# Query projection with stationary weights, an earlier start of the output projection, and an up projection ordered by weight part

## The chip, the core and the metric

The kernel runs on one core of a Trainium2 chip. A core has a matrix engine (TensorE, PE in the rows; PEld are its weight loads), a vector engine (DVE), a scalar engine (ACT), GpSimd (POOL) and a queue engine (SP) that issues the transfers from HBM. The engines run side by side and wait for each other by semaphores. The metric is the device time of one execution in microseconds (us), lower is better. A row's clock is the TensorE clock that was granted, as a share of full speed: 1.00 is 2.4 GHz, 0.50 is 1.2 GHz.

## What is computed

One decoder layer for 256 tokens of width 2048: attention in two families of heads, then an MLP, with RMS norms. Cut to what matters here:

```python
proj = rmsnorm(h, attn_norm_w) @ w_in            # 2048 -> latents, q_nsa (1024), kv (768), gates (48)
y_mla = mla_attention(c_q, c_kv, k_rope, ...)    # 8 heads, causal softmax
# nsa: 16 heads of 64; q = q_nsa.reshape(T, 2 groups, 8, 64)
s_c = q @ k_cmp.T / 8 - slope * dist             # 15 compressed blocks per group
o_c = softmax(s_c) @ v_cmp                       # "cmp"
o_s = softmax(q @ k_s.T / 8 - slope * dist) @ v_s   # "slc"; all blocks are selected at this length
o_w = softmax(q @ k_w.T / 8 - slope * dist) @ v_w   # "win"
y_nsa = g0 * o_c + g1 * o_s + g2 * o_w
h = h + concat(rmsnorm(y_mla), rmsnorm(y_nsa)) @ w_o
n = rmsnorm(h, mlp_norm_w)
h = h + square(relu(n @ w_up)) @ w_down          # 2048 -> 8192 -> 2048
return rmsnorm(h, final_norm_w)
```

## The kernel before

**Split operands.** Every large product is made in three parts. An operand is split into a rounded high part and the low rest (`w_hi`, `w_lo`; `xT[:, 0]`, `xT[:, 1]`), and the kernel adds high times high, high times low and low times high. Weights stream from HBM in chunks of 1 MB or a little less into four slots of `raw`; ACT makes `w_hi` (two slots), DVE then makes `w_lo` (two slots), and TensorE consumes the chunk. Semaphores: `hi_done` and `lo_done` count split chunks, `w_used` consumed ones, `w_half` half-consumed ones among chunks 21 to 27.

**Chunks.** Chunks 0 to 20 are the rest of the input projection and the MLA projections. Chunks 21, 23, 25, 27 (`CMP`) are the weights of the block compression. Chunks 22, 24, 26, 28, 29, 30, 31, 32 (`A_IN`) are the 1024 columns of NSA queries in `w_in`. Chunks 33 to 48 are the output projection (`WO_M` = 33 for the MLA half, `WO_N` = 41 for the NSA half), and from 49 on come the MLP's. `products` (L1199, L1200, L1203) keeps a token tile of 128 as the stationary operand and streams 512 weight columns; its result has tokens on partitions. `heads` (L1316 to L1318) does the reverse for MLA: 128 weight columns are stationary, the 256 tokens stream, and the result comes out turned, features on partitions. `up_products` (L1571, L1573) is of the second kind too: a wide matmul streams 512 columns, which are two strips of 256 (high and low part of `xT`) against `w_hi`, and a narrow one streams 256 against `w_lo`.

**Queries before.** All eight `A_IN` chunks add into PSUM banks 0 to 3 by `products`, each chunk carrying 256 rows of the weight and all 1024 columns. After chunk 32, ACT and DVE scale the two token tiles into `q_sb` (L673, L1004). TensorE then transposes it, 16 times (L1524, step `turn_q`), and ACT and DVE split each of the four banks into `q2` (L679 and L784, in turn, four times).

**Steps.** The attention is 48 steps, each a set of engine slots `("s", i)`. In slot i TensorE makes the scores of step i, transposes the probabilities of step i-3 (L1410), and multiplies those of step i-4 by the values (L1436, L1437). DVE takes the row minimum (L931) and scales the probabilities (L945, L946). ACT copies, takes exponentials, and for a finished unit writes `ysb`, `yT` and its square (L637, L639, L641); DVE adds the low part of `yT`. Steps 0 to 7 are MLA, 8 to 47 NSA (slc, win, slc, win, cmp for each pair of heads). `scores` are the 32 small products of all heads with the compressed keys (L1533, 32 columns each, into banks 2 and 3); `soft` reads them (L1015, L1016, then `cs_in`) and `weigh` finishes them. The NSA queries are needed from slot 8 on.

**Order.** `PLAN` is a list written out by the code at the top of the file that all engines run through: `("w", c)` is a chunk, `("q", (c, n))` a quarter of one (24 or, for a quarter, 6 matmuls), `("hi"/"lo", (c, half))` the splits, `("s", i)` a slot, `("k", name)` a named piece. A quarter of an output chunk is block n//2 for token tile n%2; tile 0 goes to banks 0 and 1, tile 1 to banks 2 and 3, so tile 1 has to wait for `cs_in`. The end of the attention norm (`norm_n`, L1368) goes through DVE and a chain of small POOL instructions (L416 to L419, L469) before DVE may add the first NSA half of the output projection (L970), which frees the banks for chunk 45.

**MLP.** 64 chunks of `w_up` and 64 of `w_down`; the first 8 of `w_up` are unrolled, the other 56 lie in a hardware loop of 7 rounds (`pe.Fori(1, G)`), in which 4 chunks up and 4 chunks down alternate. One up chunk is 4 banks (f) of 4 blocks (b), so 16 pairs of a wide and a narrow matmul.

## Time and profile before

| what | value |
|---|---|
| median of 3 runs | 1104.94 us (1104.5 to 1106.25) |
| the profiled execution, whole | 1105.58 us |
| its span, first to last instruction | 1103.6 us |
| PE busy | 1076.3 us (98%) |
| PE weight loads busy | 898.2 us (81%) |
| DVE, ACT, POOL busy | 635.5, 496.8, 97.4 us |
| mean granted TensorE clock | 0.993 |

The page's times are of one execution. The end of a matmul is modelled, so its busy time is no measure of how densely matmuls follow each other; for that the distance between starts in the timeline is read. A busy share is a mean over stages; the timeline and the chain of waits tell which stage waits for what. Roughly: input and MLA projections to 126 us, compression and queries with the MLA steps to 201, NSA steps with the output projection to about 346, the rest of the output projection to 380, MLP to the end.

### The profile page before, as it was taken

Reading aid. Unit: us, or ns where it says so; the run is one execution under the profiler, and the core shown is the slowest. Engines: PE = TensorE matmul, PEld = TensorE weight load, DVE = VectorE, ACT = ScalarE, POOL = GpSimd, SP = SyncE. Lnnn points to the kernel's source line nnn. Section 1 sums busy time; section 2 is a strip of 40 time slices with the busy share of each in tenths; the row PEclk is TensorE's granted clock in tenths of the full one; section 3 lists DMA queues with packets and bytes.
Section 4 is the critical chain, followed back from the end, with each engine's and each line's share of the span. In section 5 each row is a group of like instructions: output and inputs, shape, how many; then the busy total and the mean of one; then the engine's idle time right before and its main releaser. Section 6 shows DMA issues by size and latency. Waiting matters only on the chain.

```text
span 1103.6 us, 14211 instructions
## 1 busy us (share of the span) xinstructions
PE 1076.3 (98%) x5560; PEld 898.2 (81%) x5560; DVE 635.5 (58%) x781; ACT 496.8 (45%) x603; POOL 97.4 (9%) x159
## 2 busy tenths in 40 slices
PE   8999899999999999999999999999999999999996
PEld 7889787867777888888888888888888888888884
DVE  4655754677674655446545555555555654654565
ACT  4645444676654364334433433433433433443433
POOL 2136000322214000000000000000000000000003
PEclk9999999899999999999999999999999999999999
DMA  9576553142224556556555565565655555565552
GB/s 323 164 205 191 179 202 115 39 153 77 78 84 144 158 178 193 175 188 193 185 190 189 185 192 187 189 190 188 191 189 189 190 190 190 190 190 190 190 191 77
DMA packets 82977, 190.42 MB, mean 173 GB/s; under 512 B 8742, under 2 KB 21628, under 8 KB 82556
## 3 DMA queue, kind: packets, MB, share of 16 engines
q1 hardware_dynamic: 82508, 189.41, 53.9%
q10 hardware_dynamic: 432, 0.52, 0.2%
q8 instruction: 23, 0.38, 0.1%
q14 instruction: 14, 0.11, 0.0%
HBM read 187.82 MB, written 2.10 MB: 172 GB/s over the span
## 4 chain that ended last, share of the span: by engine, by line
PE 91%; DVE 5%; ACT 2%; issue 1%; DMA 0%; DVEq 0%; POOL 0%; ACTq 0%
PE ps L1571 21%; PE ps L1199 16%; PE ps L1200 16%; PE ps L1203 16%; PE ps L1573 11%; PE ps L1436 2%; DVE w_lo L784 1%; PE ps L1410 1%; ACT w_hi L529 1%; PE ps L1386 1%; PE ps L1437 1%; PE ps L1389 1%; PE ps L1385 1%; PE ps L1533 1%; PE ps L1390 1%
## 5 line engine op out<-in xcount | busy, mean ns | idle before, releaser
L784 DVE TENSOR_TENSOR w_lo<-raw,w_hi 128x2048 fp32r<-128x2048 f32 (+4 forms) x197 | 402.1, 2044 | 362.7 <-ACT w_hi L536 289.8
L536 ACT ACTIVATE w_hi<-raw 128x2048 fp32r<-128x2048 f32 x119 | 228.5, 1920 | 397.9 <-PE ps L1203 200.3
L1571 PE MATMUL ps<-xT,w_hi 128*128 128x512 f32 x1024 | 361.9, 398 | 1.3 <-DVE h_sb L970 1.0
L1573 PE MATMUL ps<-xT,w_lo 128*128 128x256 f32 x1024 | 287.4, 281 | 0.0
L1571 PEld LDWEIGHTS ps<-xT,w_hi 128*128 128x128 f32 x1024 | 192.3, 188 | 48.9 <-issue 1.3
L1573 PEld LDWEIGHTS ps<-xT,w_lo 128*128 128x128 f32 x1024 | 193.4, 189 | 0.5
L1200 PE MATMUL ps<-w_lo,hidT 128*128 128x512 f32 x448 | 174.5, 389 | 0.0
L1199 PE MATMUL ps<-w_hi,hidT 128*128 128x512 f32 x448 | 174.4, 389 | 0.0
L529 ACT ACTIVATE w_hi<-raw 128x1024 fp32r<-128x1024 f32 (+3 forms) x76 | 105.6, 1396 | 80.0 <-PE ps L1203 59.5
L1203 PE MATMUL ps<-w_hi,hidT 128*128 128x512 f32 x448 | 137.9, 389 | 0.0
L1199 PEld LDWEIGHTS ps<-w_hi,hidT 128*128 128x128 f32 x448 | 84.1, 188 | 17.7
L1203 PEld LDWEIGHTS ps<-w_hi,hidT 128*128 128x128 f32 x448 | 84.1, 188 | 17.6
L1200 PEld LDWEIGHTS ps<-w_lo,hidT 128*128 128x128 f32 x448 | 84.1, 188 | 17.0
L1199 PE MATMUL ps<-w_hi,xT 128*128 128x512 f32 (+2 forms) x184 | 68.7, 373 | 3.7 <-DVE w_lo L784 3.2
L498 POOL TENSOR_TENSOR h_sb<-h_sb,fw 128x1024 f32<-128x1024 f32 x2 | 6.2, 3111 | 724.0 <-ACT sink L745 724.0
L1200 PE MATMUL ps<-w_lo,xT 128*128 128x512 f32 (+2 forms) x184 | 65.6, 363 | 0.0
L1199 PE MATMUL ps<-w_hi,yT 128*128 128x512 f32 x128 | 55.0, 430 | 0.7 <-DVE h_sb L970 0.5
L1203 PE MATMUL ps<-w_hi,xT 128*128 128x512 f32 (+2 forms) x184 | 51.8, 363 | 0.0
L1200 PE MATMUL ps<-w_lo,yT 128*128 128x512 f32 x128 | 50.3, 393 | 0.0
L627 ACT ACTIVATE probT<-ps 128x384 f32<-128x384 f32 (+1 forms) x48 | 24.1, 502 | 53.5 <-PE ps L1410 43.1
L1199 PEld LDWEIGHTS ps<-w_hi,xT 128*128 128x128 f32 x184 | 34.5, 188 | 12.5 <-issue 4.7
L1203 PE MATMUL ps<-w_hi,yT 128*128 128x512 f32 x128 | 39.6, 391 | 0.0
(285 smaller groups left out, 1161.6 us busy)
## 6 DMA issues: line engine op xcount, KB each, us to landing
raw<-in_w_up SPq DMA_DIRECT2D x64, 1024.0 KB, 5.2
raw<-in_w_down SPq DMA_DIRECT2D x64, 1024.0 KB, 5.4
raw<-in_w_o SPq DMA_DIRECT2D x16, 1024.0 KB, 5.4
raw<-in_w_in SPq DMA_DIRECT2D x8, 1024.0 KB, 5.2
raw<-in_w_in SPq DMA_DIRECT2D x8, 816.0 KB, 4.4
raw<-in_w_in SPq DMA_DIRECT2D x7, 832.0 KB, 8.6
raw<-in_mla_w_uq SPq DMA_DIRECT2D x12, 256.0 KB, 4.3
raw<-in_mla_w_ukv SPq DMA_DIRECT2D x4, 512.0 KB, 5.2
```

The source lines that it names most:

```text
L529: act.activation(w_hi[:, split_slot(c), w0:w1], raw[:, raw_slot(c), w0:w1], ACT.Copy)\
L536: act.activation(w_hi[:, j % SPLIT, :], raw[:, j % RAW, :], ACT.Copy).then_inc(hi_done, 1)
L627: act.activation(probT[0:r, j % 2, 0:w], bank(6, w, 0, r), ACT.Copy).then_inc(pt_out, 1)
L784: return dve.tensor_tensor(dst, src, high.bitcast(F32), ALU.subtract)
L1199: pe.matmul(o, stationary(0, b, t), w_hi[:, slot, w], start=first, stop=False)
L1200: pe.matmul(o, stationary(0, b, t), w_lo[:, slot, w], start=False, stop=False)
L1203: m = pe.matmul(o, stationary(1, b, t), w_hi[:, slot, b * width + n0:b * width + n1], start=False, stop=last)
L1385: pe.matmul(o, qnT[:, h, q:q + P], knT[:, h, 0:c1 - c0], start=True, stop=False)
L1386: m = pe.matmul(o, qpT[p0:p0 + 64, h // 2, q:q + P], kpT[p0:p0 + 64, 0:c1 - c0], start=False, stop=True)
L1436: pe.matmul(o, v[0], p[:, 0:T], start=first, stop=False)
L1571: pe.matmul(ps[:, b0 + f, :].rearrange("p (c t) -> p c t", c=2), w_hi[:, slot, w], xT[:, :, k0 + b, :], start=start and b == 0, stop=False)
L1573: m = pe.matmul(ps[:, b0 + f, 0:T], w_lo[:, slot, w], xT[:, 0, k0 + b, :], start=False, stop=stop and b == 3)
```

## The change

Three things are changed.

1. **Queries.** An `A_IN` chunk is now 1024 rows (8 blocks of 128) of 256 columns, so each pair of chunks makes four heads (a "part") complete, in bank `part`. The weights are stationary and the tokens stream: `q_products` issues three matmuls of 256 columns for each of 8 blocks and 2 column groups, 48 for a chunk. The result is turned already. Since a token's scale now lies along the free axis, POOL spreads it into a square (2 copies), TensorE transposes it twice (`rows`), DVE keeps it as `rrow`; DVE scales a part out of PSUM into `qfa` or `qfb` (`scale_queries`), ACT rounds it into `q2a` or `q2b`, DVE makes the low rest (`("c", part)`). Parts 0 and 1 are done during the compression and at slot 0, parts 2 and 3 after chunk 32. `q_sb`, its 16 transposes and `turn_q` are gone. The bias tables move to other places, and two of them are made earlier.
2. **Order around slot 8.** The quarters 0 and 2 of chunk 33 (both of token tile 0) come before `scores`; `scores` comes behind slot 9, `soft` behind slot 10; the slots of steps 12 and later stand two quarters later in the plan than before, and with them `norm_n`.
3. **Up projection.** In each bank the four wide matmuls come first, then the four narrow ones, where they alternated.

```diff
@@ PLAN
-    PLAN += {CMP[1]: [("k", "rotary_k")], CMP[3]: [("k", "gelu")], A_IN[3]: [("k", "turn")]}.get(_c, [])
+    PLAN += {CMP[1]: [("k", "rotary_k"), ("k", "rows")], CMP[2]: [("c", 0)], CMP[3]: [("k", "gelu")], A_IN[3]: [("k", "turn")]}.get(_c, [])
...
-PLAN += [("k", "turn_q"), ("s", NMLA), ("k", "scores"), ("s", NMLA + 1), ("k", "soft")]
-_s = NMLA + 2
+PLAN += [("k", "out"), ("s", NMLA), ("q", (WO_M, 0)), ("hi", (WO_M + 1, 0)), ("c", 2), ("s", NMLA + 1), ("q", (WO_M, 2)),
+         ("lo", (WO_M + 1, 0)), ("c", 3), ("hi", (WO_M + 1, 1)), ("k", "scores"), ("s", NMLA + 2), ("k", "soft"), ("q", (WO_M, 1)),
+         ("lo", (WO_M + 1, 1)), ("s", NMLA + 3), ("k", "weigh"), ("q", (WO_M, 3))]
+_s = NMLA + 4
@@ chunk
-                k = 2 * A_IN.index(c)
-                return [win[:, k:k + 2, OFF_Q:OFF_B]], (2, 1024)
+                part, k = A_IN.index(c) // 2, 8 * (A_IN.index(c) % 2)
+                return [win[:, k:k + 8, OFF_Q + 256 * part:OFF_Q + 256 * part + 256]], (8, 256)
@@ DVE
+            def scale_queries(part):
+                dve.wait_ge(w_used, A_IN[2 * part + 1] + 1)
...
+                dve.tensor_tensor(queries(part)[1], pairs(bank(part)), rrow[:, :].unsqueeze(1).broadcast_to((P, 2, T)), ALU.mult).then_inc(q_in, 1)
@@ PE, new
+            def q_products(c, only):
...
+                for quarter in range(4):
...
+                    f = quarter % 2
+                    o = ps[:, part, T * f:T * f + T]
+                    for b in range(quarter // 2 * 4, quarter // 2 * 4 + 4):
+                        k = 8 * half + b
+                        w = slice(256 * b + P * f, 256 * b + P * f + P)
+                        pe.matmul(o, w_hi[:, s, w], xT[:, 0, k, :], start=k == 0 and f == 0, stop=False)
+                        m = pe.matmul(o, w_hi[:, s, w], xT[:, 1, k, :], start=False, stop=False)
...
+                        m = pe.matmul(o, w_lo[:, s, w], xT[:, 0, k, :], start=False, stop=k == KT - 1 and f == 1)
@@ up_products
                     for b in range(4):
-                        w = slice(512 * b + P * f, 512 * b + P * f + P)
-                        pe.matmul(ps[:, b0 + f, :].rearrange("p (c t) -> p c t", c=2), w_hi[:, slot, w], xT[:, :, k0 + b, :],
+                        pe.matmul(both, w_hi[:, slot, 512 * b + P * f:512 * b + P * f + P], xT[:, :, k0 + b, :],
                                   start=start and b == 0, stop=False)
-                        m = pe.matmul(ps[:, b0 + f, 0:T], w_lo[:, slot, w], xT[:, 0, k0 + b, :], start=False, stop=stop and b == 3)
+                    for b in range(4):
+                        m = pe.matmul(ps[:, b0 + f, 0:T], w_lo[:, slot, 512 * b + P * f:512 * b + P * f + P], xT[:, 0, k0 + b, :],
+                                      start=False, stop=stop and b == 3)
```

On TensorE, at the end of the MLA steps, this stood before (from the 16 transposes of `q_sb` to the start of the small products of `scores`; L1410, L1436 and L1437 are a slot's transposes and products with values, L1389 and L1390 the scores of slot 8):

```order
L1524 MATMUL ps<-ident,q_sb 128x128 [waits q_in]
L1524 MATMUL ps<-ident,q_sb 128x128 x15
L1410 MATMUL ps<-ident,prob 128x128 [waits prob_ok,pt_out]
L1410 MATMUL ps<-ident,prob 128x128 x2
L1436 MATMUL ps<-probT,v_sb 128x256 [waits y_out,pt_out]
L1437 MATMUL ps<-probT,v_sb 128x128
L1389 MATMUL ps<-k2h,q_66 128x128 [waits q_lo,score_m]
L1390 MATMUL ps<-k2l,q_66 128x128
L1389 MATMUL ps<-k2h,q_66 128x256
L1390 MATMUL ps<-k2l,q_66 128x256
L1533 MATMUL ps<-kc_102,q_66 128x32 [waits q_lo]
```

and this stands there now, from slot 9's last products (L1462, L1463) over quarter 2 of chunk 33 to the end of `scores`:

```order
L1462 MATMUL ps<-probT,v_sb 128x256 [waits y_out,pt_out]
L1463 MATMUL ps<-probT,v_sb 128x128
L1226 MATMUL ps<-w_hi,yT 128x512 [waits lo_done]
L1227 MATMUL ps<-w_lo,yT 128x512
L1226 MATMUL ps<-w_hi,yT 128x512
L1227 MATMUL ps<-w_lo,yT 128x512
L1230 MATMUL ps<-w_hi,yT 128x512 x2
L1579 MATMUL ps<-kc_102,q2a 128x32 [waits q_lo,q_in]
L1579 MATMUL ps<-kc_102,q2a 128x32 x7
L1579 MATMUL ps<-kc_102,q2a 128x32 [waits q_lo]
L1579 MATMUL ps<-kc_102,q2a 128x32 x7
L1579 MATMUL ps<-kc_102,q2b 128x32 [waits q_lo]
```

The transposes are gone, slots 8 and 9 and two quarters of the output projection stand ahead of `scores`, and its second half waits for parts 2 and 3.

On DVE, before, the eight splits of the queries stood in one row ahead of slot 8:

```order
L785 SCALAR_TENSOR_TENSOR yT<-ysb,wcols,yT 128x256 [waits y_hi]
L784 TENSOR_TENSOR q_66<-ps,q_66 64x512 [waits q_hi] x8
L931 ISA prob,nmax<-ps,bias_h 128x128 [waits bias_ok,pt_t,score_t]
L931 ISA nmax 128x1
L931 ISA prob,nmax<-ps,bias_h 128x256
```

Now the splits of parts 2 and 3 stand behind slots 8 and 9, and that of part 3 also behind half a chunk's `w_lo` (from slot 9's last instructions to slot 10's first):

```order
L961 TENSOR_SCALAR prob<-prob,scl 128x128 [waits dve_c]
L962 TENSOR_SCALAR prob<-prob,scl 128x256
L799 SCALAR_TENSOR_TENSOR yT<-ysb,wcols,yT 128x256 [waits y_hi]
L798 TENSOR_TENSOR w_lo<-raw,w_hi 128x1024 [waits half_hi]
L798 TENSOR_TENSOR q2b<-qfb,q2b 64x512 [waits q_hi] x2
L947 ISA prob,nmax<-ps,bias_odd 128x128 [waits bias_ok,pt_t,score_t]
```

The last split has moved from a place where DVE did nothing else to one where it shares the engine with a slot and a weight split.

In the up projection on TensorE the pairs of before,

```order
L1571 MATMUL ps<-xT,w_hi 128x512
L1573 MATMUL ps<-xT,w_lo 128x256
L1571 MATMUL ps<-xT,w_hi 128x512
L1573 MATMUL ps<-xT,w_lo 128x256
L1571 MATMUL ps<-xT,w_hi 128x512
L1573 MATMUL ps<-xT,w_lo 128x256
```

are now runs of four:

```order
L1617 MATMUL ps<-xT,w_hi 128x512 [waits lo_done]
L1617 MATMUL ps<-xT,w_hi 128x512 x3
L1620 MATMUL ps<-xT,w_lo 128x256 x4
L1617 MATMUL ps<-xT,w_hi 128x512 x4
L1620 MATMUL ps<-xT,w_lo 128x256 x4
```

The same matmuls are issued for a bank, with one change from wide to narrow and one back in place of four each.

## Rows read from the trace of the kernel before

**Rows 1.** The page's chain that ended last, shares of the span by engine

```profile
PE 91%; DVE 5%; ACT 2%; issue 1%; DMA 0%; DVEq 0%; POOL 0%; ACTq 0%
```

**Rows 2.** Stretches: from:to, length, busy of PE, PEld, DVE, ACT, POOL, clock, DMA, GB/s

```profile
207.20:214.00 6.80, 6.80 (x33) 6.80 (x33) 4.93 (x12) 3.90 (x11) 3.91 (x13) 0.50 0.01 2
...
427.80:1049.00 621.20, 620.84 (x3134) 526.13 (x3133) 342.13 (x201) 245.07 (x159) 0.00 (x0) 1.00 0.60 189
```

**Rows 3.** Timeline of PE, down chunk into up chunk, in the loop: start, length, what

```profile
471.56 0.39 PE L1200 MATMUL ps<-w_lo,hidT 128*128 128x512 f32 x1
...
472.24 0.39 PE L1571 MATMUL ps<-xT,w_hi 128*128 128x512 f32 x1
472.47 0.28 PE L1573 MATMUL ps<-xT,w_lo 128*128 128x256 f32 x1
472.58 0.40 PE L1571 MATMUL ps<-xT,w_hi 128*128 128x512 f32 x1
...
480.00 0.40 PE L1571 MATMUL ps<-xT,w_hi 128*128 128x512 f32 x1
```

**Rows 4.** Timeline of PE, one unrolled up chunk: its first wide matmul, the next chunk's

```profile
405.14 0.39 PE L1571 MATMUL ps<-xT,w_hi 128*128 128x512 f32 x1
...
410.68 0.39 PE L1571 MATMUL ps<-xT,w_hi 128*128 128x512 f32 x1
```

**Rows 5.** Timeline of PE in heads, first and ninth of nine matmuls

```profile
95.98 0.28 PE L1318 MATMUL ps<-cT,w_lo 128*128 128x256 f32 x1
...
96.94 0.28 PE L1317 MATMUL ps<-cT,w_hi 128*128 128x256 f32 x1
```

**Rows 6.** Timeline of PE from the transposes of the queries to the output projection

```profile
201.44 1.91 PE L1524 MATMUL ps<-ident,q_sb 128*128 128x128 f32 x16
...
205.11 0.30 PE L1389 MATMUL ps<-k2h,q 128*128 128x128 f32 x1 [0.78 <-DVE q L784]
...
207.18 6.97 PE L1533 MATMUL ps<-kc,q 128*128 128x32 f32 x32 [1.37 <-DVE q L784]
214.00 0.45 PE L1389 MATMUL ps<-k2h,q 128*128 128x128 f32 x1
...
216.77 0.77 PE L1199 MATMUL ps<-w_hi,yT 128*128 128x512 f32 x1
...
218.58 0.22 PE L1389 MATMUL ps<-k2h,q 128*128 128x128 f32 x1
...
220.01 0.48 PE L1199 MATMUL ps<-w_hi,yT 128*128 128x512 f32 x1
...
223.26 0.55 PE L1410 MATMUL ps<-ident,prob 128*128 128x128 f32 x3 [1.16 <-ACT probT L627]
...
226.59 0.55 PE L1410 MATMUL ps<-ident,prob 128*128 128x128 f32 x3 [0.67 <-ACT probT L627]
```

**Rows 7.** The chain of waits at slot 8: the first split of the queries, ACT then DVE

```profile
203.77 0.49 ACT q L679
...
204.28 0.68 DVE q L784
```

**Rows 8.** Stretches, columns as in rows 2: a slot and half a weight split, ACT's, then DVE's

```profile
222.74:226.07 3.33, 2.66 (x13) 1.96 (x13) 2.01 (x2) 3.30 (x10) 0.74 (x1) 1.00 0.00 0
224.06:227.57 3.51, 2.84 (x16) 1.87 (x15) 3.44 (x11) 3.48 (x11) 0.74 (x1) 1.00 0.00 0
```

**Rows 9.** Timeline about norm_n: its sum, the last POOL instruction, the add behind

```profile
345.79 0.60 PE L1368 MATMUL ps<-ones,sqacc 128*128 128x1 f32 x4 [0.57 <-POOL sqacc L464]
...
353.13 1.06 POOL L469 COPY root_w<-rn 128x2 f32<-128x2 f32 x1
...
354.88 1.28 DVE L970 SCALAR_TENSOR_TENSOR h_sb<-ps,rn,h_sb 128x1024 f32<-128x1024 f32 x1 [0.73 <-PE ps L1203]
```

**Rows 10.** Timeline of POOL, the MLA norm: first and last of the same chain

```profile
243.60 0.19 POOL L416 TENSOR_TENSOR root_w<-rm 128x2 f32<-128x2 f32 x1 [1.21 <-DVE rm L805]
...
248.01 0.18 POOL L469 COPY root_w<-rm 128x2 f32<-128x2 f32 x1
```

More of the change, by code:

```diff
@@ L100, in _step @@
         return [("k", "norm_n")] if s == len(STEPS) + LAG + 1 else []
-    return [("s", s)] + ([("k", "weigh")] if s == NMLA + 3 else [])
-for _c in range(WO_M, WO_N + 4):
+    return [("s", s)]
+for _c in range(WO_M + 1, WO_N + 4):
     if _c in (WO_M + 4, WO_N):
@@ L1000, in _ @@
                     dve.tensor_copy(vcmp[:, :, :], ps[0:NC, 7, 64:64 + NG * DK].rearrange("p (g d) -> p g d", g=NG)).then_inc(k_ok, 1)
[L1001 to L1010 removed]
+                elif i == "rows":
+                    dve.wait_ge(rr_t, 1)
+                    dve.tensor_copy(rrow[:, :], bank(7, T)).then_inc(rr_ok, 1)
+                    dve.wait_ge(rr_ok, 1)
+                elif i == "out":
+                    for part in (2, 3):
+                        scale_queries(part)
+                elif kind == "c":
+                    if i < 2:
+                        scale_queries(i)
+                    high, full = queries(i)
+                    for e in range(2):
+                        r, other = slice(64 * e, 64 * e + 64), slice(64 - 64 * e, 128 - 64 * e)
+                        dve.wait_ge(q_hi, 2 * i + e + 1)
+                        low(high[other, e, :, :], full[r, :, :], high[r, e, :, :]).then_inc(q_lo, 1)
                 elif i == "soft":
@@ L1392, in slot @@
             def slot(i):
[L1393 to L1394 removed]
+                score(i)
                 j = i - LAG
```

120 lines of the change are left out of this document (66 added, 54 removed).

## The prediction

> **What bounds the kernel now.** Read the chain that ended last first: TensorE is 91% of it, a transfer none [rows 1]. Then the stretches: in the MLP loop, 621.2 us of the 1103.6 us span, TensorE is busy for 620.8 us at the full clock, with DVE at 342 and ACT at 245 us beside it [rows 2]. So in the loop the time is the number of matmuls times their spacing, and an edit there counts only if it changes the spacing. The timeline about slot 8 is the other kind of place: TensorE waits for the splits of the queries, then makes the 32 small products of `scores` at the half clock, 0.50 [rows 2, 6]. The change touches both kinds, and makes the query chunks longer for it. The sum below is made against the profiled execution, 1105.58 us, which is 0.6 us over the median.
>
> **1. Up projection, in the loop.** A pair of a wide and a narrow matmul takes 0.353 us there: 22 pairs from 472.24 to 480.00 [rows 3]. Four pairs are 1.411 us. Unrolled, the same pairs take 0.346: 16 of them from 405.14 to 410.68 [rows 4], 1.385 for four. What do runs of four take? A wide matmul after a wide one takes 0.227 (three from 471.56 to 472.24) [rows 3]; a narrow one after a narrow one, each with its own 128 weight columns, takes 0.120 (eight from 95.98 to 96.94) [rows 5]. So 4 x 0.227 + 4 x 0.120 = 1.387, which is what the unrolled code already has. The loop's pairs are 0.0065 us dearer than their parts, and the pair right after a down chunk is not: 472.24 to 472.58, 0.340 [rows 3]. I read this as a price of changing the width again and again, which a bank would now pay once. The loop has 56 chunks of 4 banks, 224 banks: (1.411 - 1.387) x 224 = -5.4 us. If the one change from wide to narrow and back is as cheap as that first pair, a bank takes 3 x 0.227 + 3 x 0.120 + 0.340 = 1.380, -6.9 us; if the extra stays with each pair, 0. The unrolled 8 chunks give nothing (1.385 against 1.387). I take -5.4, since both parts of that sum are measured spacings of the same shapes. All of it is on the path; nothing else runs out of cover, as DVE and ACT have 45% and 60% of the loop idle [rows 2].
>
> **2. Query chunks.** Before, 8 chunks of 24 matmuls of 512 columns at 0.227: 43.6 us. Now 8 chunks of 48 of 256 columns at 0.120: 46.1 us, +2.5 us on the path. The spacing is that of `heads`, which has the same triple of matmuls [rows 5]; the lower end is the unrolled pair's 0.346 less a wide 0.227, 0.119 [rows 3, 4], +2.1; nothing among the rows is dearer for this shape unrolled. The two transposes of `rows` replace part of the 16 taken away: 16 took 1.75 us up to the next instruction (their modelled end gives 1.91) [rows 6], so two cost +0.2. The splits of parts 0 and 1 cost nothing: ACT and DVE need some 3 us for each, behind which only a weight split is queued whose chunk starts later than that; the tight one is part 1, ahead of slot 0 and the split of chunk 30, which I work out to end about 0.8 us early. If that cover goes it costs under 1 us. The new transfers have 1 KB pieces as the compression weights have; TensorE has weights in stock.
>
> **3. Around slot 8.** I lay the new order on the old times, from 201.44, where slot 7 ends [rows 6]. A NSA slot takes 1.43 us (218.58 to 220.01) [rows 6], and a quarter, six wide matmuls at 0.227, some 1.4 (216.77 to 218.58, 1.8 us, is partly at the low clock). TensorE: slot 8 to 202.9, quarter to 204.3, slot 9 to 205.8, quarter to 207.2, then 24 of the 32 small products at the transposes' 0.109 (1.75 / 16) [rows 6] to 209.9. ACT is free at 203.77, where the first split began [rows 7]; a slot and half a weight split take it 3.3 us [rows 8], to 207.1; part 2 takes 2 x 0.49 to 208.0; DVE follows with 2 x 0.68 [rows 7], to 208.9, in time. DVE then has its slot and half a weight split, 3.4 us [rows 8], before part 3: 212.3, and 2 x 0.68 more, 213.7 at worst, 213.3 as I chain them, since a part of that 3.4 was slowed beside ACT. So the last 8 small products wait from 209.9 to 213.3: a new idle stretch of 3.4 us. They and slot 10 end at 215.6. Then quarter 1 of chunk 33 waits for `cs_in`. Before, 3.24 us lay between slot 9's end and the first quarter that needs `cs_in` (216.77 to 220.01), and a quarter and slot 10 filled them [rows 6]. Now slot 10 stands ahead, the quarters of tile 0 are spent, and nothing fills them: idle until 218.8.
> Against the 220.01 of before that is 1.2 us earlier, with one more quarter done (1.5 us), and the two waits behind, 1.16 and 0.67 [rows 6], have gone with the pile-up on ACT. At the full clock: -4.5 us.
> The clock takes most of it back. Before, TensorE did little between 203.9 and 207.2; from 207.20 to 214.00 the granted clock is 0.50, the lower of its two levels (1.2 GHz), and 6.8 us of the small products without a gap did not bring it up again [rows 2, 6]. The new order has little work from 207.2 to 218.8: small products, 3.4 us idle, one slot, 3.2 us idle. So I expect it at the low level from about the first idle stretch until some microseconds of chunk 33 are done. 8 small products and slot 10 (0.9 + 1.4) then take twice as long, +2.3, and the first 3 to 4 us of real work cost another 1.7: +4.0, between 2.3 and 5.7. Net -0.5 us.
> The Trainium skill ("TensorE: Matmul & The Clock Gate", Why this matters for your kernels) warns of idle gaps between bursts of matmuls as what throttles the engine. The rows agree in kind. Its advice would count the small products as work that keeps the engine warm, which the stretch at 0.50 does not show; if it held, the +4.0 would go, which is rival C.
>
> **4. The NSA norm.** `norm_n` now stands two quarters (2.7 us) nearer to chunk 45. Before, from its sum at 345.79 to the last POOL instruction's end at 354.19 it took 8.4 us, and DVE's add began at 354.88, held by TensorE, not by POOL [rows 9]. With 2.7 us less in between, TensorE is done first and waits for POOL and the first add, 1.28 us [rows 9]: 8.4 + 1.3 = 9.7 against some 7.2 us of its own, 2.5 us of waiting where 0.4 was, +2.1 at the upper end. The same chain for MLA took 4.6 us (243.60 to 248.19) [rows 10], where the NSA one took 7.1 of its 8.4; with that, no more than before: 0. A mean of the two is +0.9, and I take that.
>
> **Sum.** -5.4 + 2.5 + 0.2 - 0.5 + 0.9 = -2.3 us on 1105.58, so 1102.6 us against the median of 1104.94.
>
> **Rivals.**
> A, the order in the up projection doesn't matter: what makes the loop's pairs dearer belongs to each pair or each narrow matmul in a loop. For it: the loop and the unrolled code issue the same instructions, and only the loop pays [rows 3, 4], so the width is not the only suspect. Against it: the pair after a down chunk, 0.340. Then term 1 is 0 and the rest +3.1: 1108.0 us.
> The Trainium skill ("TensorE: Matmul & The Clock Gate", Back-to-back issue gap) gives a matmul's spacing as its columns over the clock and a fixed 2.5 ns, whatever stands before it; by that rule the order is free, as in A. The fixed part that the rows show is larger, 0.227 - 0.213 = 0.014 us, and it changes between the loop and the unrolled code, so the rule is not the whole of it here.
> B, slower: reading two strips is what costs. A wide matmul of the up projection would keep its spacing to the next instruction, 0.236 in the loop (480.00 and the pairs before it, 0.353 less 0.117) and 0.230 unrolled, also after a wide one, and the narrow ones would come at 0.120 instead of 0.117. A bank: 4 x 0.236 + 3 x 0.120 + 0.117 = 1.421, +0.010 x 224 = +2.2 us, and +0.3 unrolled; with the rest, 1110.5 us. It decides from a wide-to-wide spacing above 0.234 on, where the gain of the runs is spent. Against it: 472.24 to 472.47, a two-strip matmul at 0.23 [rows 3].
> C, the clock holds through the new idle stretches: 4.0 us less than my sum, 1098.6 us. For it: each stretch is hardly longer than 3 us, with work between. Against it: before, a stretch with 1.6 us of idling and 0.8 of waiting was enough [rows 6].
>
> **How the numbers follow.** The forecast 43%, A 22%, B 13%, C 15%, something else 7%. About 2.2 us (0.2%) is what a measurement of this kernel can tell from no change. My forecast lies at that edge, with 1.5 us of error either way: 50 to 50 for faster and same. C is faster; A is half slower, half same; B is slower; the rest is split. Faster 0.22 + 0.15 + 0.03 = 0.40, same 0.21 + 0.08 + 0.02 = 0.31 and slower 0.14 + 0.13 + 0.02 = 0.29. The range goes from C with the cheapest first pair (-1.5) to B: 1097 to 1110.5; the forecast's own range is 1100 to 1105.
>
> **What would show it.** In the timeline of the loop: wide after wide at 0.227 (B: 0.236), narrow after narrow at 0.120, a bank at 1.387 us. In the query chunks 48 matmuls at 0.120. About slot 8: an idle stretch of about 3.4 us inside the small products that DVE's split of part 3 ends, another of about 3.2 us that `cs_in` ends, and a granted clock of 0.50 over part of it. Ahead of chunk 45 a wait for DVE of 0.4 to 2.5 us. I am wrong if the loop's narrow matmuls come at more than 0.125 us in their runs, if a weight split falls behind during the query chunks, or if the clock stays low beyond chunk 33.

## The result, and the profile after

The changed kernel takes 1107.2 us (median of 15 runs, 1105.93 to 1108.15) against 1105.04 us (15 runs, 1104.5 to 1106.25). The ratio is 1.0018, 95% interval 1.0011 to 1.0025. It is slower by 2.2 us, where I had forecast 2.3 us less. The value lies inside my range, on the wrong side of zero.

The two profiled executions differ by 1.9 us in span (1103.6 and 1105.5). The same places in the program, by the start of the instruction on TensorE (us):

| place | before | after | difference | added since the last place |
|---|---|---|---|---|
| first chunk of weights | 16.03 | 16.57 | +0.54 | +0.54 |
| end of slot 7 | 201.44 | 203.92 | +2.48 | +1.94 |
| chunk 45 | 356.31 | 359.79 | +3.48 | +1.00 |
| first matmul of the MLP | 381.10 | 384.60 | +3.50 | +0.02 |
| last matmul | 1092.56 | 1094.39 | +1.83 | -1.67 |

The first line holds nothing of the change; it is how late the first chunk could begin in these executions (between 15.4 and 16.8 us in the traces of the changed kernel and its variants). So the attention part lost 3.0 us where the forecast had 2.5 + 0.2 - 0.5 + 0.9 = 3.1, and the MLP gave back 1.7 us where the forecast had 5.4. That the 3.0 is so near the 3.1 is luck: its terms were off by 0.4 to 0.8 us each, and the errors cancel (see "Why the prediction was wrong").

**The query chunks.** The timeline of PE in chunk 32 (start and length in us, engine, line, operation, out<-in, shapes, count), a matmul and the ninth after it; 1.08 us for nine, 0.120 each. Inside the query chunks the mean is 0.1197 us, and 0.2290 for the 512 columns before. At 11 places, where one query chunk or another piece of work follows, the distance to the next start is longer, about 0.20 now and 0.32 before. From start to start the 384 matmuls take 46.95 us and the 192 of before took 45.00, so the change costs 1.95 us here:

```profile
199.78 0.28 PE L1482 MATMUL ps<-xT,w_lo 128*128 128x256 f32 x1
...
200.86 0.28 PE L1482 MATMUL ps<-xT,w_lo 128*128 128x256 f32 x1
```

**Around slot 8.** The timeline of PE; in square brackets is the idle time ahead of an instruction and what ended it. It answers to [rows 6]:

```profile
209.70 1.85 PE L1579 MATMUL ps<-kc,q2a 128*128 128x32 f32 x16
211.64 1.06 PE L1579 MATMUL ps<-kc,q2b 128*128 128x32 f32 x8
217.24 1.89 PE L1579 MATMUL ps<-kc,q2b 128*128 128x32 f32 x8 [4.54 <-DVE q2b L798]
218.97 0.45 PE L1416 MATMUL ps<-k2h,q2a 128*128 128x128 f32 x1
...
221.46 0.63 PE L1463 MATMUL ps<-probT,v_sb 128*128 128x128 f32 x2
224.97 0.47 PE L1226 MATMUL ps<-w_hi,yT 128*128 128x512 f32 x1 [2.88 <-DVE pc L1043]
```

Both idle stretches of the forecast are there: one inside the small products, ended by DVE's split of part 3 (4.54 us, 3.4 forecast), one for `cs_in` (2.88 us, 3.2 forecast). What DVE and ACT did meanwhile, from their timelines: ACT splits part 3 behind slot 9, and DVE has a weight split in front of it.

```profile
213.22 1.26 ACT L693 ACTIVATE q2b<-qfb 64x512 fp32r<-64x512 f32 x2
```

```profile
214.55 1.21 DVE L798 TENSOR_TENSOR w_lo<-raw,w_hi 128x1024 fp32r<-128x1024 f32 x1
215.78 1.40 DVE L798 TENSOR_TENSOR q2b<-qfb,q2b 64x512 fp32r<-64x512 f32 x2
```

Stretches of the same place and of the loop (from:to, length, busy of PE, PEld, DVE, ACT and POOL, granted clock, DMA share, GB/s), as in [rows 2]:

```profile
209.70:217.24 7.54, 2.92 (x26) 2.72 (x24) 6.83 (x14) 5.73 (x13) 5.09 (x9) 0.88 0.00 0
217.24:224.97 7.73, 4.85 (x19) 4.40 (x20) 3.25 (x12) 2.56 (x8) 0.73 (x1) 0.68 0.00 0
427.80:1049.00 621.20, 620.90 (x3149) 528.35 (x3148) 342.83 (x203) 245.28 (x160) 0.00 (x0) 1.00 0.60 190
```

**The loop.** TensorE is as full as before, 620.9 of 621.2 us. The timeline from a down chunk into an up chunk shows what its matmuls cost, to be set against [rows 3]:

```profile
475.61 0.61 PE L1230 MATMUL ps<-w_hi,hidT 128*128 128x512 f32 x2
476.06 1.07 PE L1617 MATMUL ps<-xT,w_hi 128*128 128x512 f32 x4
476.97 0.64 PE L1620 MATMUL ps<-xT,w_lo 128*128 128x256 f32 x4
477.44 1.09 PE L1617 MATMUL ps<-xT,w_hi 128*128 128x512 f32 x4
478.37 0.63 PE L1620 MATMUL ps<-xT,w_lo 128*128 128x256 f32 x4
478.84 0.40 PE L1617 MATMUL ps<-xT,w_hi 128*128 128x512 f32 x1
```

The first four wide matmuls follow a down chunk, whose matmuls are as wide: 476.06 to 476.97, 0.227 each, as forecast. The next four follow narrow ones: 477.44 to 478.37, 0.233 each. The narrow ones take 0.1175. A bank of eight takes 1.402 us in the loop and 1.403 in the unrolled chunks from the fourth on, where I had 1.387. Before, it took 1.4125 in the loop and 1.387 unrolled. So 224 x (1.4125 - 1.402) - 32 x (1.402 - 1.387) = 2.35 - 0.48 = 1.9 us gained, where the forecast had 5.4.

### The profile page after: what moved, and what is told of

It reads as the page before. It is cut to its first block, busy times and chain, and to the rows that moved or that the text cites. A ratio compares the mean times of both kernels' runs of the same rounds, so it can differ in the third digit from the quotient of the medians.

```text
span 1105.5 us, 14583 instructions
## 1 busy us (share of the span) xinstructions
PE 1074.4 (97%) x5738; PEld 906.5 (82%) x5738; DVE 638.5 (58%) x785; ACT 495.1 (45%) x602; POOL 96.8 (9%) x161
## 4 chain that ended last, share of the span: by engine, by line
PE 91%; DVE 5%; ACT 2%; issue 1%; DMA 0%; POOL 0%; DVEq 0%; ACTq 0%
PE ps L1617 21%; PE ps L1226 15%; PE ps L1227 14%; PE ps L1230 14%; PE ps L1620 11%; PE ps L1462 2%; DVE w_lo L798 2%; PE ps L1478 1%; PE ps L1479 1%; PE ps L1482 1%; PE ps L1436 1%; PE ps L1463 1%; PE ps L1413 1%; PE ps L1416 1%; ACT w_hi L546 1%
## 5 line engine op out<-in xcount | busy, mean ns | idle before, releaser
L1617 PE MATMUL ps<-xT,w_hi 128*128 128x512 f32 x1024 | 279.5, 394 | 1.3 <-DVE h_sb L986 1.0
L1617 PEld LDWEIGHTS ps<-xT,w_hi 128*128 128x128 f32 x1024 | 175.9, 189 | 26.1 <-issue 1.3
L1620 PEld LDWEIGHTS ps<-xT,w_lo 128*128 128x128 f32 x1024 | 157.1, 189 | 21.7
L1620 PE MATMUL ps<-xT,w_lo 128*128 128x256 f32 x1024 | 162.8, 281 | 0.0
L1226 PE MATMUL ps<-w_hi,xT 128*128 128x512 f32 x120 | 42.7, 356 | 1.9 <-DVE w_lo L798 1.5
L1227 PE MATMUL ps<-w_lo,xT 128*128 128x512 f32 x120 | 40.6, 348 | 0.0
L1478 PE MATMUL ps<-xT,w_hi 128*128 128x256 f32 x128 | 37.1, 290 | 1.7 <-DVE w_lo L798 1.7
L1226 PEld LDWEIGHTS ps<-w_hi,yT 128*128 128x128 f32 x128 | 24.0, 187 | 16.1 <-issue 12.4
```

Source lines behind the costliest of these rows:

```text
L1226: pe.matmul(o, stationary(0, b, t), w_hi[:, slot, w], start=first, stop=False)
L1227: pe.matmul(o, stationary(0, b, t), w_lo[:, slot, w], start=False, stop=False)
L1478: pe.matmul(o, w_hi[:, s, w], xT[:, 0, k, :], start=k == 0 and f == 0, stop=False)
L1617: pe.matmul(both, w_hi[:, slot, 512 * b + P * f:512 * b + P * f + P], xT[:, :, k0 + b, :], start=start and b == 0, stop=False)
L1620: m = pe.matmul(ps[:, b0 + f, 0:T], w_lo[:, slot, 512 * b + P * f:512 * b + P * f + P], xT[:, 0, k0 + b, :], start=False, stop=stop and b ...
```

## Experiments

Times are medians; a ratio is to the kernel before, run on the same chip beside it (1105.2 to 1105.3 us), with its 95% interval. Where there is one run, the time is that run's, and the spacings of its trace are what counts.

### Which part of the change did what

**The new up projection in the kernel before.**

```diff
                     for b in range(4):
-                        w = slice(512 * b + P * f, 512 * b + P * f + P)
-                        pe.matmul(ps[:, b0 + f, :].rearrange("p (c t) -> p c t", c=2), w_hi[:, slot, w], xT[:, :, k0 + b, :],
-                                  start=start and b == 0, stop=False)
-                        m = pe.matmul(ps[:, b0 + f, 0:T], w_lo[:, slot, w], xT[:, 0, k0 + b, :], start=False, stop=stop and b == 3)
+                        pe.matmul(both, w_hi[:, slot, 512 * b + P * f:512 * b + P * f + P], xT[:, :, k0 + b, :],
+                                  start=start and b == 0, stop=False)
+                    for b in range(4):
+                        m = pe.matmul(ps[:, b0 + f, 0:T], w_lo[:, slot, 512 * b + P * f:512 * b + P * f + P], xT[:, 0, k0 + b, :],
+                                      start=False, stop=stop and b == 3)
```

> The kernel before with the new up projection alone (four wide matmuls, then four narrow ones). The changed kernel's trace has a bank of eight matmuls at 1.402 us in the loop and unrolled, against 1.4125 and 1.387 before. If that is the up projection's own (theory), this kernel shows the same spacings and gains 224 x 0.0107 - 32 x 0.0147 = 1.9 us: 1103.1 us. Rival: the spacing depends on what the query change did to the placement of other work; then wide after wide is at 0.227 as I forecast, and the gain is about 5 us: 1100.

Measured: 1103.65 us, ratio 0.9985 (0.9976 to 0.9994), that is 1.7 us less, with a bank at 1.402 in the loop. The up projection's share is its own.

**The rest of the change without it** (the same edit, the other way, on the changed kernel).

> The changed kernel with the old up projection, so the query chunks, the order about slot 8 and the norm alone. If the parts add up (theory): 1107.2 + 1.9 = 1109.1 us, +4.1 over before, of which the traces show some 2.0 in the query chunks, 0.2 about slot 8 and 0.9 at the two norms. Rival: part of the loss is the up projection's, and this one stands at 1108 or below.

Measured: 1108.8 us, ratio 1.0032 (1.002 to 1.0044), 3.5 us more. The two parts add up: -1.7 + 3.5 = +1.8, for 1.0018 x 1105 = +2.0 measured.

### Why a wide matmul after a wide one took 0.233 and not 0.227

My rival B had been that reading two strips of `xT` costs. Three runs take the layout and the form of the moving operand away as causes, a fourth the target.

**Strips next to each other, in the changed kernel and in the one before.**

```diff
-        xT, Y_AT = seq(X_AT, ("xT", [P, 2, KT, T], F32R))
+        xT_blocks, Y_AT = seq(X_AT, ("xT", [P, KT, 2, T], F32R))
+        xT = xT_blocks[:, :, :, :].rearrange("p k c t -> p c k t")
```

> The changed kernel with the high and the low part of a block of xT side by side in memory, so that a wide matmul reads 512 adjacent columns and not two strips of 256 lying 16 KB apart. The arithmetic and the order are the same. Theory (reading two strips costs): wide after wide falls from 0.233 to the 0.227 of the down projection, a bank to 4 x 0.227 + 4 x 0.1185 = 1.382 us, and the time by 256 x 0.020 = 5.1 us to 1102.1. Rival (the cost lies in the stationary side or in a change of width): the spacings stay, 1107.2.

> The kernel before with the same layout of xT: adjacent parts, the old order of a wide and a narrow matmul in turn. Theory (two strips cost, in the old order too): a wide to its narrow one takes 0.227 instead of 0.236 (loop) and 0.230 (unrolled), a pair 0.344, and the time falls by 896 x 0.0093 + 128 x 0.003 = 8.7 us to 1096.3. Rival (alternating widths costs in the loop, whatever the strips): the pair stays at 0.353 in the loop, 1105.0. Between them, a pair at 0.347 as unrolled: 1099.

Measured: 1106.8 us, ratio 1.0018 (1.0009 to 1.0027), the same as the changed kernel's; and 1105.07 us, ratio 0.9998 (0.9989 to 1.0007). The timeline of PE in the loop of the first, with 0.2325 for a wide one (476.88 to 477.81) and 0.1175 for a narrow one:

```profile
476.40 0.64 PE L1621 MATMUL ps<-xT,w_lo 128*128 128x256 f32 x4
476.88 1.09 PE L1618 MATMUL ps<-xT,w_hi 128*128 128x512 f32 x4
477.81 0.63 PE L1621 MATMUL ps<-xT,w_lo 128*128 128x256 f32 x4
478.28 1.09 PE L1618 MATMUL ps<-xT,w_hi 128*128 128x512 f32 x4
```

I had expected 5 and 9 us. Nothing moved: where the strips lie is free, in both orders.

**The access written with one dimension.**

```diff
-                        pe.matmul(both, w_hi[:, slot, 512 * b + P * f:512 * b + P * f + P], xT[:, :, k0 + b, :],
-                                  start=start and b == 0, stop=False)
+                        pe.matmul(ps[:, b0 + f, :], w_hi[:, slot, 512 * b + P * f:512 * b + P * f + P],
+                                  xT_blocks[:, k0 + b, :, :].rearrange("p c t -> p (c t)"), start=start and b == 0, stop=False)
```

> The changed kernel with xT's parts adjacent, as in the run before, and the wide matmul written with one dimension of 512 columns, source and target, instead of two of 256. Adjacent parts alone changed no spacing. Theory (the two-dimensional access costs, not where the strips lie): wide after wide 0.227, a bank 1.38 us, 1102. Rival (the moving side is innocent): 0.233 and 1.402 stay.

Measured: 1106.38 us (one run), a bank at 1.402. The rival holds.

**Banks in turn.**

```diff
-                for f in range(4):
-                    if free is not None:
+                if free is not None:
+                    for f in range(4):
                         free(f)
-                    both = ps[:, b0 + f, :].rearrange("p (c t) -> p c t", c=2)
-                    for b in range(4):
+                for b in range(4):
+                    for f in range(4):
+                        both = ps[:, b0 + f, :].rearrange("p (c t) -> p c t", c=2)
                         pe.matmul(both, w_hi[:, slot, 512 * b + P * f:512 * b + P * f + P], xT[:, :, k0 + b, :],
                                   start=start and b == 0, stop=False)
-                    for b in range(4):
+                    for f in range(4):
```

> The changed kernel with the block loop outside and the bank loop inside: four wide matmuls into four different banks, then four narrow ones. Theory (adding to the same bank four times in a row is what makes the wide ones 0.233 instead of 0.227): wide after wide 0.227, four of each 1.38 us, 1102. Rival (the target is innocent): 1.402 stays and the time is that of the changed kernel.

Measured: 1109.97 us (one run), and 1.402 for eight matmuls again. The target is innocent too. This order costs something else: all four banks have to be free at a chunk's start, so the first chunk of the MLP waits longer (2.25 us, against 0.95 in the changed kernel), and the clock was at 0.50 behind that wait. Timeline and stretch:

```profile
385.75 2.04 PE L1618 MATMUL ps<-xT,w_hi 128*128 128x512 f32 x4 [2.25 <-DVE h_sb L986]
```

```profile
385.75:389.15 3.40, 3.40 (x10) 2.92 (x11) 2.08 (x1) 0.00 (x0) 0.00 (x0) 0.50 0.70 246
```

**Runs of two and of sixteen.** Both on the kernel with slot 8 reordered (below, 1098.85 us). For two (1 is a wide matmul, 0 a narrow one, the second number its block):

```diff
+                    for wide, b in ((1, 0), (1, 1), (0, 0), (0, 1), (1, 2), (1, 3), (0, 2), (0, 3)):
```

and for sixteen, which ends the loop over the banks behind the wide ones and starts it anew:

```diff
                     for b in range(4):
                         pe.matmul(both, w_hi[:, slot, 512 * b + P * f:512 * b + P * f + P], xT[:, :, k0 + b, :],
                                   start=start and b == 0, stop=False)
+                for f in range(4):
                     for b in range(4):
```

> The kernel with slot 8 reordered, the up projection in runs of two: two wide, two narrow, four times over two banks' worth. Theory (each wide matmul that follows a wide one costs 0.006 us more than the 0.227 of the down projection, and what follows a width change is at its plain cost): a bank has two such places instead of three, 1.396. Rival (the loop makes every change of width dearer, as in the old order): with four changes instead of two a bank comes near the middle between 1.402 and 1.4125, 1.407.

> The same base, a chunk as sixteen wide matmuls and then sixteen narrow ones. If a wide matmul after a wide one is what costs: 16 x 0.233 + 16 x 0.1185 = 5.62 us for a chunk against 5.607 of runs of four, so 1099.7 us. Rival (a change of width costs): 5.58, 1097.5.

Measured: 1095.96 us and a bank at 1.393; 1095.26 us and a bank at 1.390 (one run each). Both theories fall, since runs of four are the dearest of the three; the 1.396 that I had for runs of two was near, but by a cause that the sixteen refute (5.56 us for a chunk, 5.62 expected). The chunk of sixteen shows why. The start-to-start distances in it, in ns, from the trace of a chunk that follows narrow matmuls:

```
wide    233 236 228 233 231 227 227 227 227 227 227 227 227 227 227 227
narrow  113 119 120 120 120 120 120 120 120 120 120 120 120 120 120 120
```

After some five matmuls the plain spacings of my forecast are there, 0.227 and 0.120. Right behind the change from narrow to wide, five wide ones take 26 ns more together, and right behind the change back the first two narrow ones take 8 ns less. The four wide ones of a run of four all lie in the dear stretch. So the extra belongs to the change of width, as I had read it in the kernel before, but not to one matmul.

A change of width is also a change from `w_hi` to `w_lo` as the source of the weights. That alone costs nothing here: in the query chunks and in the down chunks the two alternate at one width, and the spacing stays at 0.120 and 0.227.

What is not explained is the run of two. By adding up these distances (233 + 236 wide, 113 + 119 narrow, twice) it would cost 1.402 a bank, like four. It costs 1.393: in its trace a bank goes 234 235 (wide), 116 113 (narrow), 232 231 (wide), 113 120 (narrow). Why short runs get cheaper again stays open.

**Runs of sixteen in the changed kernel itself.**

> The changed kernel with its order about slot 8 as it was, and runs of sixteen in place of runs of four. In the run with slot 8 reordered the first five wide matmuls of a run took 0.233, 0.236, 0.228, 0.233 and 0.231 and the rest 0.227, the first narrow one 0.113 and from the third on 0.120. Theory (a change of width disturbs the next five matmuls or so, and a run of four lies inside that): the same here, a bank at 1.390 instead of 1.402, so 256 x 0.0115 = 2.9 us off: 1104.3 us. Rival (the gain seen there came with the other slot 8): no gain, 1107.2.

Measured: 1103.82 us, ratio 0.9989 (0.998 to 0.9998), 3.4 us under the changed kernel (2.9 expected). The timeline of PE in the loop: sixteen wide in 484.19 - 480.54 = 3.65 us, 0.228 each, and sixteen narrow in 1.92 us, 0.120 each.

```profile
480.54 3.82 PE L1617 MATMUL ps<-xT,w_hi 128*128 128x512 f32 x16
484.19 2.08 PE L1621 MATMUL ps<-xT,w_lo 128*128 128x256 f32 x16
486.11 1.09 PE L1617 MATMUL ps<-xT,w_hi 128*128 128x512 f32 x4
```

### Why the same pairs cost more in the loop than unrolled

**TensorE's loop written out, with the old order in turn and with runs of four.** The other engines keep their loops; the base is slot 8 reordered.

```diff
-            with pe.Fori(1, G) as g:
+            for g in range(1, G):
                 for j in range(GC):
```

> The kernel with slot 8 reordered (1098.85 us), the old up projection (wide and narrow in turn), and TensorE's own MLP loop written out seven times; the other engines keep theirs. Theory (the loop itself makes alternating matmuls dearer, 1.4125 a bank against 1.387 unrolled): all 256 banks at 1.387, so 256 x 0.0147 = 3.8 us less than with runs of four: 1095.1 us. Rival (the place in the program matters, say that up chunks stand among down chunks there, not the loop): the pairs stay at 0.353 and the time is 1098.85 + 1.9 = 1100.8.

> The same with the new up projection (runs of four). In the changed kernel runs of four take 1.402 in the loop and unrolled alike, so theory: nothing changes, 1098.9 us. Rival (a loop costs something at its jumps): a few tenths of a us less.

Measured: 1099.85 us (ratio 0.9951, 0.9937 to 0.9964), 1.0 us over the looped kernel with runs of four; and 1097.88 us, one run, with a bank at 1.402 as in the loop. The timeline of PE of the first has 35 pairs early in the MLP from 399.12 to 411.25, 0.3466 us each:

```profile
399.12 0.39 PE L1617 MATMUL ps<-xT,w_hi 128*128 128x512 f32 x1
...
411.25 0.39 PE L1617 MATMUL ps<-xT,w_hi 128*128 128x512 f32 x1
```

and 26 pairs where the loop was, from 467.60 to 476.77, 0.353 each, though no loop is left:

```profile
467.60 0.39 PE L1617 MATMUL ps<-xT,w_hi 128*128 128x512 f32 x1
...
476.77 0.40 PE L1617 MATMUL ps<-xT,w_hi 128*128 128x512 f32 x1
```

So the loop is not the cause: the pairs are as dear in the same place without it. The distances (ns, wide then narrow) show repeating patterns for one and the same sequence of instructions:

```
in the chunks of the loop, before    236 113 | 232 118 | 241 120 | 236 113 | ...   mean 353.3 a pair
first and third up chunk, before     230 117 | 230 116 | 230 117 | ...             mean 346.7
second up chunk, before              233 117 | 231 112 | 233 117 | 231 113 | ...   mean 346.5
first up chunk, written-out kernel   236 113 | 233 117 | 241 120 | ...             mean 353.3
```

The last line is the same place as the second, behind the same idle stretch, and it fell into the dear pattern. A pattern keeps itself up until something else than pairs comes, or a wait: in the first round of the loop of before, ahead of any down chunk, the pairs behind a wait of 0.36 us already run at 0.354 (5.661 us for the chunk at 439.15).

**Another beginning.** In a chunk's first bank the first four matmuls are two wide, two narrow; the rest goes in turn.

> Slot 8 reordered and wide and narrow in turn, as in the kernel before, but in a chunk's first bank the first two pairs are two wide and then two narrow ones. In the traces with the order in turn the same pairs repeat at 0.3533 us behind a down chunk and mostly at 0.3467 behind transposes or an idle stretch, unrolled or not. Theory (what stands ahead of the first pairs sets the rhythm, and it then keeps itself up): after another beginning some chunks of the loop keep another mean than 0.3533 to their end. Rival (the place among down chunks sets it): 0.3533 again after the first four matmuls.

Measured: 1099.54 us (one run). In the loop the pairs go back to 0.353 after the changed four, in 54 of its 56 chunks. The two others are in its first round: the second, behind a wait, falls into the cheap pattern, and the third keeps it to its end, 5.558 us from 433.91 to 439.47, where the kernel before has 5.661:

```profile
433.91 0.63 PE L1621 MATMUL ps<-xT,w_hi 128*128 128x512 f32 x2
...
439.47 0.63 PE L1621 MATMUL ps<-xT,w_hi 128*128 128x512 f32 x2
```

In the unrolled chunks 4 to 8, where the order in turn ran at 5.547 us a chunk, it now runs at 5.647. So what stands ahead can choose the pattern, in both directions, and my theory holds there; but no chunk behind a down chunk left the dear one, so the rival holds for those. What chooses it stays open.

### Around slot 8

**Part 3 split early.**

```diff
-PLAN += [("k", "out"), ("s", NMLA), ("q", (WO_M, 0)), ("hi", (WO_M + 1, 0)), ("c", 2), ("s", NMLA + 1), ("q", (WO_M, 2)),
-         ("lo", (WO_M + 1, 0)), ("c", 3), ("hi", (WO_M + 1, 1)), ("k", "scores"), ("s", NMLA + 2), ("k", "soft"), ("q", (WO_M, 1)),
+PLAN += [("k", "out"), ("s", NMLA), ("q", (WO_M, 0)), ("c", 2), ("c", 3), ("hi", (WO_M + 1, 0)), ("s", NMLA + 1), ("q", (WO_M, 2)),
+         ("lo", (WO_M + 1, 0)), ("hi", (WO_M + 1, 1)), ("k", "scores"), ("s", NMLA + 2), ("k", "soft"), ("q", (WO_M, 1)),
```

> The changed kernel with the splits of query part 3 right behind those of part 2, ahead of the split of chunk 34 and of slot 9 on ACT and DVE. The changed kernel idles 4.54 us ahead of the last 8 small products and 2.88 us for cs_in. Theory (each engine's queue order makes the two stretches): the first goes, DVE reaches soft some 6 us earlier, near 219, and TensorE idles some 4 us for cs_in instead; the first quarter of tile 1 starts at 219 instead of 225. With the clock as low as before that is 5 to 6 us: 1101.5. Rival (it only moves: slot 9 and its split are late instead, and the waits come back behind slot 10): 1105 or more.

Measured: 1102.3 us, ratio 0.9975 (0.9966 to 0.9984), 4.9 us under the changed kernel. The waits of PE from slot 8 to the norm (who, what, line, for whom; us in total, times, longest) have one long one left:

```profile
PE ps L1226 <- DVE pc L1043: 5.1, 1, 5.1
```

It had been 2.88: of the 4.54 us that went, 2.2 came back here.

**And soft ahead of slot 10.**

```diff
-         ("lo", (WO_M + 1, 0)), ("hi", (WO_M + 1, 1)), ("k", "scores"), ("s", NMLA + 2), ("k", "soft"), ("q", (WO_M, 1)),
+         ("hi", (WO_M + 1, 1)), ("k", "scores"), ("k", "soft"), ("lo", (WO_M + 1, 0)), ("s", NMLA + 2), ("q", (WO_M, 1)),
```

> As the last, and soft ahead of slot 10, with the first half split of chunk 34 on DVE behind it. Theory: cs_in at about 215.5, some 1 us behind the end of slot 10 on TensorE; both idle stretches go (7.4 us), and with them most of the low clock, whose cost I count from the changed kernel's rows as 3.5 us: 1107.2 - 7.4 - 3.5 = 1096.3, and 1100 if half of it returns as waits for probT, since DVE and ACT then have slot 9, slot 10 and soft behind the splits. If the clock falls whatever the idling is (rival): 1100 at best.

Measured: 1098.85 us, ratio 0.9944 (0.993 to 0.9957), 8.4 us under the changed kernel, between the 1096.3 and the 1100 of the theory. The timeline of PE and the stretch over it:

```profile
209.21 1.85 PE L1579 MATMUL ps<-kc,q2a 128*128 128x32 f32 x16
210.91 1.94 PE L1579 MATMUL ps<-kc,q2b 128*128 128x32 f32 x16
212.70 0.31 PE L1416 MATMUL ps<-k2h,q2a 128*128 128x128 f32 x1
...
215.80 0.47 PE L1226 MATMUL ps<-w_hi,yT 128*128 128x512 f32 x1 [1.41 <-DVE pc L1043]
...
218.10 0.55 PE L1436 MATMUL ps<-ident,prob 128*128 128x128 f32 x3 [0.23 <-ACT probT L644]
...
221.82 0.47 PE L1226 MATMUL ps<-w_hi,yT 128*128 128x512 f32 x1 [1.05 <-DVE w_lo L798]
```

```profile
205.00:226.00 21.00, 18.31 (x111) 15.32 (x110) 19.62 (x53) 17.57 (x46) 12.45 (x23) 1.00 0.10 34
```

7.42 us of idling have become 2.7, and the granted clock stays 1.00 in this execution. Chunk 45 starts at 350.75 us instead of 359.79, slot 8 at 203.43 instead of 203.92: 8.55 us less between them, 4.7 of it idling and the other 3.8, by subtraction, the low clock. That was worth 3.5 in my count from the rows. The order does not secure the clock, though: of the seven profiled kernels with it, three hold 1.00 here and four have 6.8 us at 0.50, and two of the five runs of this kernel, at 1099.1 and 1099.52 us, have a mean clock of 0.993 to 0.994 where the other three have 0.996. In all seven TensorE idles at most 2.7 us here.

### The fastest kernel

**Mirrored chunks.** Slot 8 reordered, runs of sixteen, and in every second chunk the narrow ones first (the block's first matmul, which starts the bank, is a wide one of an even chunk).

```diff
+                order = ((1, 0), (0, 1))[k0 // 4 % 2]
+                for wide in order:
                     for f in range(4):
```

> Slot 8 reordered and runs of sixteen, but every second chunk has the narrow ones first, so that runs of 32 stand next to each other and half of the width changes go. By the theory of the last run a chunk gains half of the 14.6 ns that it stands above 16 x 0.227 + 16 x 0.120: 64 x 0.0073 = 0.5 us, so 1094.8 us against 1095.3 of one run of sixteen. If that is so it is the fastest kernel of this study. Rival (what precedes a run matters in another way, as the three rhythms of the alternating order show): chunks with the narrow ones first differ from 5.56 by more than 0.02 us.

Measured: 1094.99 us, ratio 0.9908 (0.9893 to 0.9924). In its trace 32 narrow and then 32 wide matmuls stand in a row with one dear stretch for both chunks (chunks of 5.539 and 5.575 us, mean 5.557 where one run of sixteen had 5.560 in the loop). That gain over runs of sixteen, 0.2 us by the spacings and 0.3 by the times, is too small to be told from none; the 10.2 us under the kernel before are not.

## Why the prediction was wrong, point by point

**Term 1, the up projection: -5.4 forecast, -1.9 by the spacings, -1.7 alone on the chip.** This is the step that failed: "4 x 0.227 + 4 x 0.120 = 1.387". Both spacings were right for what they were read from, and the new order reaches them, but only in long runs. I took them for properties of a shape. They are properties of a matmul among its like: 0.227 came from the down chunks, where nothing but wide ones stands for 5 us, and 0.120 from `heads`, narrow ones only. A price of changing the width was in my text, as paid once for a bank by the first matmul. It is spread over the matmuls that follow, +26 ns over the five wide ones and -8 ns over the first two narrow ones, and a run of four has no wide matmul that is free of it. So each of the 256 banks takes 1.402 and not 1.387, 3.8 us in all. What in the engine makes this price stays open. In runs of sixteen the gain is (1.4125 - 1.390) x 224 = 5.0 us, and with the unrolled chunks 4.9. That the 0.227 us of wide after wide in [rows 3] stood behind a whole chunk of wide ones was to be seen.

**The unrolled chunks.** I had them at zero; they lost 0.5 us, by the same cause.

**Rival B** had the spacing of wide after wide nearly right, 0.233 for 0.236, by the wrong mechanism (and its bank of 1.421 measured 1.402): strips, their distance, the dimensions of the access and the bank were each changed without any effect. **Rival A** falls too: in the loop the new order gained 0.0105 us a bank, and others more. The formula of the Trainium skill ("TensorE: Matmul & The Clock Gate", Back-to-back issue gap), columns over the clock and a fixed 2.5 ns, which the page gives for an isolated matmul, does not cover it: for the same 3072 columns a bank took 1.387 and 1.4125 (in turn), 1.393 (twos), 1.402 (fours) and 1.390 (sixteens).

**Term 2, the query chunks: +2.7 with the row transposes, +1.9 measured.** The spacing was right, 0.120. The 512-column matmuls before were at 0.2290 here, not 0.227, and the sum left out the longer distances at the edges of the chunks, so the old chunks were 1.4 us dearer than I had them and the new ones 0.9. The first splits stayed covered.

**Term 3, slot 8: -0.5 forecast, +0.15 measured** (+1.00 up to chunk 45, less 0.43 and 0.42 at the two norms). The mechanism was right in each step: the two idle stretches, who ends them, and the low clock, 10.2 us of it in the profile, at a cost of some 3.8 by the subtraction under "Around slot 8" (4.0 forecast), so rival C falls. The first stretch was 4.54 and not 3.4, and that came on DVE. Part 2 was split by 211.6, as chained (208.9 and the 2.5 us by which slot 7 ends later). Then its slot and half a weight split took 4.2 us up to 215.78 and not 3.4, and the split of part 3 1.4 where I had let 1.0 count. Of the slot, three instructions were slow, 0.57, 0.82 and 0.72 us, where the next slot has 0.16, 0.35 and 0.48 for the same lines:

```profile
212.37 0.57 DVE L959 TENSOR_TENSOR scl<-scl,gates 128x2 f32<-128x2 f32 x1
...
213.17 0.82 DVE L962 TENSOR_SCALAR prob<-prob,scl 128x256 f32<-128x256 f32 x1
213.91 0.72 DVE L799 SCALAR_TENSOR_TENSOR yT<-ysb,wcols,yT 128x256 fp32r<-128x256 f32 x1
```

POOL was at work beside all three and hardly beside those of the next slot, but also beside L961 at 212.97, which took its usual 0.29 us; no run tests whether that is the cause.

The times of the changed kernel spread over 2.2 us and those of the kernel before over 1.8, 0.8 without one run. In the traces of the six kernels with the changed order about slot 8 the low clock there lasts 10.2 us in two and 13.7 in four, in those with the old order 10.2 in all three; that may be the larger spread, but one profile for each kernel does not show it.

**Term 4, the NSA norm: +0.9 forecast, +0.43 measured.** TensorE waits 0.71 us in front of chunk 45 for DVE, and DVE 1.16 us for POOL, as said:

```profile
358.36 2.48 DVE L986 SCALAR_TENSOR_TENSOR h_sb<-ps,rn,h_sb 128x1024 f32<-128x1024 f32 x2 [1.16 <-POOL root_w L480]
```

```profile
359.79 0.47 PE L1226 MATMUL ps<-w_hi,yT 128*128 128x512 f32 x1 [0.71 <-DVE h_sb L986]
```

Its POOL chain took 6.8 us from the sum at 351.55 to 358.32; the 8.4 of before held time in which nobody waited.

**What I had not seen: the MLA norm, +0.42.** One shift in the order puts a weight split of DVE ahead of its copy of the sum, on which TensorE waits. First the kernel before, then after:

```profile
242.94 0.16 DVE L956 TENSOR_SCALAR ssq<-ps 128x2 f32<-128x2 f32 x1 [0.81 <-PE ps L1368]
```

```profile
247.58 1.42 DVE L798 TENSOR_TENSOR w_lo<-raw,w_hi 128x1024 fp32r<-128x1024 f32 x1
...
248.92 0.15 DVE L972 TENSOR_SCALAR ssq<-ps 128x2 f32<-128x2 f32 x1
...
249.12 0.65 PE L1462 MATMUL ps<-probT,kv_sb 128*64 128x256 f32 x2 [0.68 <-DVE ssq L972]
```

I had followed the queue order past `norm_n`, where the diff moves something, and not past the other norm, which only moves because everything behind slot 8 does.

**The sum.** Forecast -5.4 + 2.7 - 0.5 + 0.9 = -2.3; measured -1.7 + 1.9 + 0.15 + 0.43 + 0.42 = +1.2 in the profiles, the late first chunk (+0.54) aside, and +2.2 in the medians. With the late first chunk it would be +1.7; the rest I can't place. The errors of terms 2, 3 and 4 and the norm that I had left out (-0.8, +0.65, -0.5, +0.4) nearly cancel, by luck: the sum missed by 3.5 us and term 1 alone by 3.7. In the chances, A should have given 0.11 each to same and slower, as its text says, and not 0.08 and 0.14.

## What to carry to other kernels

Read the spacing of a matmul where its neighbours are those of the new order; a spacing from a uniform stretch holds for the inside of long runs only, so where widths must alternate, measure the lengths of run that the banks allow: here sixteen cost 1.390 a bank, two 1.393, four 1.402, and strict alternation 1.387 or 1.4125. A gain that is found on one engine's queue (here 8.4 us by moving two splits and a softmax past each other, four times the whole effect of the change) is seen by writing down, for each idle stretch, what stands in front of its releaser. When a slot in a written-out order shifts, go through all later meeting points of two engines, not only those that the diff names.

## What the runs showed of the hardware that I had not expected

A fixed sequence of alternating 512- and 256-column matmuls repeats in one of several patterns, at 0.3467 or at 0.3533 us a pair, for up to some 220 matmuls on end, with identical instructions and no wait; what precedes can switch it, a loop has no part in it.

Where the moving operand lies (two strips 16 KB apart or adjacent), how many dimensions its access has, and whether successive matmuls add to one bank or to four in turn changed no mean spacing by as much as 1 ns.

The clock falls without a long idle stretch too. In the kernel with the written-out loop and the order in turn, the list of waits of TensorE names none between slot 8 and the MLA norm, and yet the clock went to 0.50 at 213.04 us, during the last of the 32 small products, for this stretch:

```profile
213.04:219.86 6.82, 6.82 (x26) 6.06 (x26) 6.58 (x18) 4.77 (x13) 3.02 (x4) 0.50 0.00 0
```

In the profile of the kernel of 1098.85 us, with the same code there, it held at 1.00. In the kernel with the banks in turn, 3.4 us at 0.50 followed an idle stretch of 2.25 us ahead of the MLP; behind the 0.95 us at that place in the changed kernel it stayed at 1.00.
